# Hybrid streaming encoder step on one core: the first key and value block in another order, its weights and cached latents in smaller parts

## What is computed

```python
for l in range(DEPTH):                        # two layers; 256 prompt + 64 sample tokens
    h = rmsnorm(x, norm_mix[l]);  proj = h @ w_in[l]
    c_kv = rmsnorm(kv_lat)                    # new latents, 256 wide
    lat_all = concat([cache_latent, c_kv])    # sample stream: 512 cached rows, then 64 new
    kv = (lat_all @ w_kvup).reshape(.., 8, 64 + 64)   # per head: key part and value
    k = rmsnorm(concat([k_nope, k_rope])) * gain      # QK-norm over 96
    # attention over k and v, two other mixers, gated merge, SwiGLU
```

## Time and profile before

| What | Value |
|---|---|
| Median of 3 runs | 1054.91 us |
| Lowest and highest run | 1054.8 and 1055.82 us |
| Span of the profiled execution (the page gives no other time of it) | 1054.5 us |
| PE busy | 1046.4 us, 99% |
| DVE, ACT, POOL busy | 642.1, 503.9, 307.8 us |

### The profile page before, as it was taken

How to read it: one execution, slowest core, us unless ns; L and a number is a source line. 1 busy time by engine, 2 the same in 40 slices (tenths; PEclk the granted TensorE clock), 3 DMA queues, 4 the chain that set the end, 5 groups by cost and what they waited for, 6 DMA issues and landing times.

```text
span 1054.5 us, 20034 instructions
## 1 busy us (share of the span) xinstructions
PE 1046.4 (99%) x7594; PEld 1007.3 (96%) x7594; DVE 642.1 (61%) x1075; ACT 503.9 (48%) x915; POOL 307.8 (29%) x262
## 2 busy tenths in 40 slices
PE   8999999999999999999999999999999999999998
PEld 6899988999999999999988999989999999999998
DVE  6768764445766665643567786554457566565444
ACT  6456655444544434434354475544445444443342
POOL 2366555541121111100122755546312111111000
PEclk9999999999999999999999999999999999999999
DMA  7455433244435545454514544333355355454443
GB/s 246 117 157 147 152 96 119 94 133 148 149 113 178 159 140 153 146 181 144 177 41 137 146 146 128 99 120 104 117 160 161 120 161 158 142 156 143 156 149 122
DMA packets 49283, 147.98 MB, mean 140 GB/s; under 512 B 8865, under 2 KB 14593, under 8 KB 49217
## 3 DMA queue, kind: packets, MB, share of 16 engines
q1 hardware_dynamic: 42992, 144.76, 44.3%
q10 hardware_dynamic: 6224, 2.30, 0.9%
HBM read 143.82 MB, written 3.22 MB: 139 GB/s over the span
## 4 chain that ended last, share of the span: by engine, by line
PE 94%; DVE 3%; ACT 1%; POOL 1%; issue 1%; DMA 0%; SPq 0%; POOLq 0%; DVEq 0%; ACTq 0%
PE psum L551 28%; PE psum L553 28%; PE psum L552 28%; PE psum L703 1%; PE psum L743 1%; PE psum L726 1%; PE psum L662 1%; PE psum L734 1%; PE psum L775 1%; PE psum L663 1%; PE psum L667 1%; PE psum L950 0%; PE psum L826 0%; PE psum L641 0%; DMA raw<-w_all 0%
## 5 line engine op out<-in xcount | busy, mean ns | idle before, releaser
L551 PE MATMUL psum<-AH,WH 128*128 128x320 f32 x1328 | 415.7, 313 | 0.2
L553 PE MATMUL psum<-AH,WL 128*128 128x320 f32 x1328 | 410.3, 309 | 0.0
L552 PE MATMUL psum<-AL,WH 128*128 128x320 f32 x1328 | 410.3, 309 | 0.0
L551 PEld LDWEIGHTS psum<-AH,WH 128*128 128x128 f32 x1328 | 249.3, 188 | 7.9 <-issue 5.5
L552 PEld LDWEIGHTS psum<-AL,WH 128*128 128x128 f32 x1328 | 249.4, 188 | 0.7
L553 PEld LDWEIGHTS psum<-AH,WL 128*128 128x128 f32 x1328 | 249.3, 188 | 0.0
L1032 ACT CAST WH<-raw 128x1024 fp32r<-128x1024 f32 x167 | 174.0, 1046 | 137.2 <-PE psum L553 135.5
L1450 DVE TENSOR_TENSOR WL<-raw,WH 128x1024 fp32r<-128x1024 f32 x104 | 128.8, 1240 | 121.1 <-ACT WH L1032 120.7
L1897 POOL TENSOR_TENSOR WL<-raw,WH 128x1024 fp32r<-128x1024 f32 x61 | 149.7, 2468 | 130.1 <-ACT WH L1032 113.9
L1633 DVE TENSOR_TENSOR WL<-raw,WH 128x1024 fp32r<-128x1024 f32 x88 | 107.6, 1223 | 49.6 <-ACT WH L1195 48.2
L1902 POOL TENSOR_TENSOR fab<-fa,fb 128x320 f32<-128x320 f32 x44 | 38.7, 880 | 270.1 <-DVE fb L1638 270.1
(11 more groups left out here) (250 smaller groups left out, 1568.5 us busy)
## 6 DMA issues: line engine op xcount, KB each, us to landing
raw<-w_all SPq DMA_DIRECT2D x267, 512.0 KB, 3.5
y_out<-X SPq DMA_DIRECT2D x8, 160.0 KB, 3.0
X<-x_in SPq DMA_DIRECT2D x2, 320.0 KB, 5.5
X<-x_in SPq DMA_DIRECT2D x1, 640.0 KB, 7.2
lat_out<-ckv ACTq DMA_DIRECT2D x2, 320.0 KB, 2.9
scratch<-brel SPq DMA_DIRECT2D x8, 63.8 KB, 4.5
ckv<-lat_in SPq DMA_DIRECT2D x1, 384.0 KB, 5.5
bias<-scratch SPq DMA_DIRECT2D x8, 48.0 KB, 4.4
```

The source lines that it names most:

```text
L551: mm(out, WH[:, slot, c0:c0 + cols], high, start=first, stop=False)
L552: mm(out, WH[:, slot, c0:c0 + cols], low, start=False, stop=False)
L553: return mm(out, WL[:, slot, c0:c0 + cols], high, start=False, stop=last)
```

## The change

In block 0 of layer 0 the value rows come ahead of the key rows on PE, and their unit is loaded first, in two transfers of 512 columns. The cached rotary keys are issued ahead of the key unit, and the cached latents come in three parts (128, 128 and 256 rows) in place of two (128 and 384). ACT casts both units of `w_kvup` in halves (the key unit by its contraction halves, in strides), and PE waits for each half apart. DVE makes the value unit's low part in halves and the key unit's whole, then raises `split_ready` by two with a small memset. The third part of the latents is cast by ACT and subtracted by DVE after the keys of block 0. Unit 2 is cast by POOL (`first_cast`) in place of ACT, between the rotary parts of blocks 0 and 1. POOL's low part of unit 2 comes after block 1's rotary part, where it stood ahead of it. Layer 1 keeps its order and its two parts.

```diff
--- before.py
+++ after.py
@@ -111,6 +111,10 @@
 HALF = 64
 
 
+LATENTS = (((0, 128), (128, 256), (256, PAST)), ((0, 128), (128, PAST)))
+CKV0 = (0, 4)
+
+
 def fresh(kb):
 
     return slice(0 if kb < KB - 1 else HALF, 128)
@@ -476,11 +483,14 @@
     def _(sp):
         lat = lat_in[0:1].rearrange("a p c n -> (a p) c n")
         sp.dma_start(ckv[:, :, T:T + 128], lat[:, :, 0:128]).then_inc(s.cache_lat[0], 16)
+        sp.dma_start(raw[:, 1, 0:512], w_all[stored(1)][:, 0:512]).then_inc(s.first_raw, 16)
+        sp.dma_start(raw[:, 1, 512:1024], w_all[stored(1)][:, 512:1024]).then_inc(raw_ready[1], 16)
+        sp.dma_start(krT[64:96, T:NKEY], kr_in[0:1].rearrange("a p n -> (a p) n")).then_inc(s.cache_kr, 16)
         sp.dma_start(raw[:, 0, :], w_all[stored(0)]).then_inc(raw_ready[0], 16)
-        sp.dma_start(raw[:, 1, :], w_all[stored(1)]).then_inc(raw_ready[1], 16)
         sp.dma_start(cst[:, K_ID:K_ID + 128], cst_in[:, K_ID:K_ID + 128]).then_inc(s.id_in, 16)
-        sp.dma_start(krT[64:96, T:NKEY], kr_in[0:1].rearrange("a p n -> (a p) n")).then_inc(s.cache_kr, 16)
-        sp.dma_start(ckv[:, :, T + 128:NKEY], lat[:, :, 128:PAST]).then_inc(s.cache_lat[1], 16)
+        for n in (1, 2):
+            c0, c1 = LATENTS[0][n]
+            sp.dma_start(ckv[:, :, T + c0:T + c1], lat[:, :, c0:c1]).then_inc(s.cache_lat[n], 16)
         sp.dma_start(par[:, 0:DEPTH * NPAR], par_in).then_inc(s.par_in, 16)
         sp.dma_start(X[:, 0:2, :], x_in[:, 0:2, :]).then_inc(s.x_in[0], 16)
         sp.dma_start(raw[:, 2, :], w_all[stored(2)]).then_inc(raw_ready[2], 16)
@@ -643,25 +653,31 @@
 
         def key_rows(l, kb):
 
-            if kb == 0:
+            if kb == 0 and l > 0:
                 pe.wait_ge(s.high_ready, l * NU + U_KVK + 1)
                 pe.wait_ge(s.x_ready, 16 * l + 5)
-                pe.wait_ge(s.ckv_ready, 3 * l + 1)
+                pe.wait_ge(s.ckv_ready, CKV0[l] + 1)
             elif kb == 1:
                 pe.wait_ge(s.x_ready, 16 * l + 7)
-                pe.wait_ge(s.ckv_ready, 3 * l + 2)
+                pe.wait_ge(s.ckv_ready, CKV0[l] + 2)
             elif kb == CACHED:
                 pe.wait_ge(s.tile_free, l * NT + T_QL + 2)
-                pe.wait_ge(s.ckv_ready, 3 * l + 3)
-            elif kb != CACHED + 1:
+                pe.wait_ge(s.ckv_ready, CKV0[l] + len(LATENTS[l]) + 1)
+            elif kb > CACHED + 1 or 1 < kb < CACHED:
                 pe.wait_ge(s.kn_ready, l * KB + kb - 1)
+            if kb == 2:
+                pe.wait_ge(s.ckv_ready, CKV0[l] + len(LATENTS[l]))
             out = psum[:, kbank(kb), :]
             keys = slice(KEY0[kb], KEY0[kb] + 128)
             wh, wl = (w[:, U_KVK, :].rearrange("k (p c n) -> k c p n", p=4, c=2) for w in (WKH, WKL))
             for c in range(2):
+                if l == kb == 0:
+                    pe.wait_ge(s.first_high, 3 + c)
                 mm(out, ckvH[:, c, keys], wh[:, c], start=c == 0, stop=False)
                 mm(out, ckvL[:, c, keys], wh[:, c], start=False, stop=False)
-            if kb == 0:
+            if l == kb == 0:
+                pe.wait_ge(s.first_low, 3)
+            elif kb == 0:
                 pe.wait_ge(s.split_ready, l * NU + U_KVK + 1)
             for c in range(2):
                 last = mm(out, ckvH[:, c, keys], wl[:, c], start=False, stop=c == 1)
@@ -669,7 +685,9 @@
 
         def value_rows(l, kb):
 
-            if kb == 0:
+            if l == kb == 0:
+                pe.wait_ge(s.ckv_ready, 1)
+            elif kb == 0:
                 pe.wait_ge(s.high_ready, l * NU + U_KVV + 1)
                 pe.wait_ge(s.x_ready, 16 * l + 6)
             elif kb == 1:
@@ -681,11 +699,15 @@
             out = psum[:, kbank(kb) + 1, :]
             keys = slice(KEY0[kb], KEY0[kb] + 128)
             for c in range(2):
+                if l == kb == 0:
+                    pe.wait_ge(s.first_high, 1 + c)
                 mm(out, ckvH[:, c, keys], WKH[:, U_KVV, c * 512:c * 512 + 512], start=c == 0, stop=False)
                 mm(out, ckvL[:, c, keys], WKH[:, U_KVV, c * 512:c * 512 + 512], start=False, stop=False)
-            if kb == 0:
+            if kb == 0 and l > 0:
                 pe.wait_ge(s.split_ready, l * NU + U_KVV + 1)
             for c in range(2):
+                if l == kb == 0:
+                    pe.wait_ge(s.first_low, 1 + c)
                 last = mm(out, ckvH[:, c, keys], WKL[:, U_KVV, c * 512:c * 512 + 512], start=False, stop=c == 1)
             last.then_inc(s.v_full, 1)
 
@@ -862,8 +884,12 @@
         for l in range(DEPTH):
 
             for kb in range(CACHED):
-                key_rows(l, kb)
-                value_rows(l, kb)
+                if l == kb == 0:
+                    value_rows(l, kb)
+                    key_rows(l, kb)
+                else:
+                    key_rows(l, kb)
+                    value_rows(l, kb)
                 if kb == 0:
                     turn_rope(l, 0)
                 else:
@@ -1049,7 +1075,7 @@
 
         def cached_high(l, part):
 
-            keys = (slice(T, T + 128), slice(T + 128, NKEY))[part]
+            keys = slice(*(T + c for c in LATENTS[l][part]))
             act.wait_ge(s.cache_lat[part], 16 * l + 16)
             nc.scalar.copy(ckvH[:, :, keys], ckv[:, :, keys]).then_inc(s.ckv_cache_high, 1)
 
@@ -1205,20 +1231,30 @@
         gain_pairs = par_in.rearrange("p (l c) -> p l c", c=NPAR)[:, :, C_GQ:C_GQ + 2]
         for row, at_row in ((96, 80), (112, 64)):
             act.dma_start(gains[row:row + 16], gain_pairs[at_row:at_row + 16]).then_inc(s.gains_in, 16)
-        high(0, U_KVK)
-        high(0, U_KVV)
+        act.wait_ge(s.first_raw, 16)
+        nc.scalar.copy(WKH[:, U_KVV, 0:512], raw[:, U_KVV, 0:512]).then_inc(s.first_high, 1)
+        act.wait_ge(raw_ready[U_KVV], 16)
+        nc.scalar.copy(WKH[:, U_KVV, 512:1024], raw[:, U_KVV, 512:1024]).then_inc(s.first_high, 1)
+        act.wait_ge(raw_ready[U_KVK], 16)
+        for c in range(2):
+            h_, r_ = (w.rearrange("k (p c n) -> k c p n", p=4, c=2)[:, c] for w in (WKH[:, U_KVK, :], raw[:, U_KVK, :]))
+            nc.scalar.copy(h_, r_).then_inc(s.first_high, 1)
+        cached_high(0, 1)
 
         for l in range(DEPTH):
             if l > 0:
                 for k in range(4, KC):
                     norm_chunk(l, 0, k, square=False)
             for kb in range(CACHED):
-                key_square(l, kb)
-                if l == 0 and kb == 0:
-                    cached_high(0, 1)
-                elif l == 0 and kb < 3:
-                    high(l, U_KV + kb - 1)
-                value_copy(l, kb)
+                if l == kb == 0:
+                    value_copy(l, kb)
+                    key_square(l, kb)
+                    cached_high(0, 2)
+                else:
+                    key_square(l, kb)
+                    if l == 0 and kb == 2:
+                        high(l, U_KV + 1)
+                    value_copy(l, kb)
                 if kb == 0:
                     rope_rows(l, 0)
                     if l == 0:
@@ -1451,8 +1487,8 @@
 
         def cached_low(l, part):
 
-            keys = (slice(T, T + 128), slice(T + 128, NKEY))[part]
-            dve.wait_ge(s.ckv_cache_high, 2 * l + part + 1)
+            keys = slice(*(T + c for c in LATENTS[l][part]))
+            dve.wait_ge(s.ckv_cache_high, len(LATENTS[0]) * l + part + 1)
             TT(ckvL[:, :, keys], ckv[:, :, keys], ckvH[:, :, keys].bitcast(F32), ALU.subtract).then_inc(s.ckv_ready, 1)
 
         def full_tile(l, t):
@@ -1642,8 +1678,15 @@
         v.memset(ssum[:], 0.0).then_inc(s.warm_zero, 1)
         v.memset(par[:, DEPTH * NPAR:(DEPTH + 1) * NPAR], 0.0).then_inc(s.x_ready, KC)
         cached_low(0, 0)
-        low(0, U_KVK)
-        low(0, U_KVV)
+        for c in range(2):
+            half = slice(512 * c, 512 * c + 512)
+            dve.wait_ge(s.first_high, 1 + c)
+            TT(WKL[:, U_KVV, half], raw[:, U_KVV, half], WKH[:, U_KVV, half].bitcast(F32), ALU.subtract) \
+                .then_inc(s.first_low, 1)
+        dve.wait_ge(s.first_high, 4)
+        TT(WKL[:, U_KVK, :], raw[:, U_KVK, :], WKH[:, U_KVK, :].bitcast(F32), ALU.subtract).then_inc(s.first_low, 1)
+        dve.wait_ge(s.first_low, 3)
+        v.memset(small[:, 30:31], 0.0).then_inc(s.split_ready, 2)
         cached_low(0, 1)
 
         for l in range(DEPTH):
@@ -1652,6 +1695,8 @@
             TT(kgain[0:QK], col(C_GK, l, slice(0, QK)), col(C_GQ, l, slice(0, QK)), ALU.mult)
             for kb in range(CACHED):
                 key_scale(l, kb)
+                if l == kb == 0:
+                    cached_low(0, 2)
                 if kb == 0:
                     dve.wait_ge(s.gains_in, 32)
                     TT(kgain[QK:ROWS], gains[QK:ROWS, l, 1:2], gains[QK:ROWS, l, 0:1], ALU.mult).then_inc(s.gains, 1)
@@ -1897,6 +1942,11 @@
             g_.tensor_tensor(WL[:, u % RING, :], raw[:, u % RING, :], WH[:, u % RING, :].bitcast(F32), ALU.subtract) \
                 .then_inc(s.split_ready, 1)
```

(10 more changed lines are left out.)

5 lines of the change are left out of this document (4 added, 1 removed).

## The result

The changed kernel takes 1058.32 us in the median of 7 runs (1057.81 to 1059.8), the kernel before 1055.27 (1054.8 to 1056.65, 7 runs). The ratio is 1.003, with a 95% interval of 1.002 to 1.0039: slower by about 3 us, where I had forecast 0.5 us less and given slower 0.05. The forecast of 1054.4 and its range (to 1055.6) are both missed.

A forecast was written before the change was run, and what follows sets the result against it. PE was taken as the bound, busy 1046.4 of 1054.5 us. A lead of 1.0 at block 1's turn, cut to 0.5 by block 2's, gave 1054.0, plus 0.4: median 1054.4, range 1053.2 to 1055.6.

The forecast's parts named there:

- The opening decides, and PE's start of the dense part is the measure: Whole kernel: the change is worth what it moves PE's dense start at 24.47; some 1.8 us to be had.
- given back later: Rival, first dense part: PE waits there for ACT's squares or POOL's sums, giving 1054.9, no change; chance 0.11.
- `Kn` of block 1 comes at 16.74 - 0.4 + 0.65 = 17.0: DVE before block 1's sum: the 256-row latent part makes `Kn` 0.25 us later than before.
- it starts at 20.2: DVE's low part of unit 3 waits for POOL's low part of unit 2, starting at 20.2 instead of 19.45.
- I cost that at nothing: First dense product: low parts of `x` come up to 0.75 us later, costed at nothing, up to 0.5 without cover.
- The split costs two or three issues, but they lie 4 us ahead of the landing: Opening transfers: splitting adds no delay, and the key unit lands near 7.7.
- the key unit lands late: Rival, opening: a landing from 8.2 on makes the kernel slower, 1056.0 at half rate; chance 0.13.
- the base: Span to time: sum made against the profiled span of 1054.5, carrying 0.4 us up to the median.
- a lead of 1.3 at block 1: PE, block 1: with smaller latent parts it starts near 11.2 in place of 12.52.
- POOL's cast: Unit 2 on POOL: 1.7 us, covered by a wait; rival that it is slow gives 1057.0, chance 0.05.
- The 256-row latent part: DVE behind `Kn` of block 0: 512 elements, about 0.65 us, done by 14.9 ahead of PE's 15.35.
- The clock rises late: Rival, opening: PE's pauses keep 1.2 GHz through block 1, costing 2.8 us there, result 1055.8; chance 0.07.

The follow-up runs named there:

- run 12: Kernel before with cached latents in three parts, POOL's low part behind block 1's rotary keys, DVE's gain product and `AL` moved: 1054.74 us, ratio 0.9993.
- run 5: Changed kernel with `AL` 0 and 1 alone moved behind unit 3's low part on DVE: 1057.12 us, ratio to before 1.0013.
- run 6: Kernel before with POOL's low part of unit 2 moved behind block 1's rotary part: 1055.47 us, ratio 1.0.
- run 4: Changed kernel with DVE's second gain product moved ahead of block 0's keys and `AL` 0 and 1 behind unit 3's low part: 1055.94 us.
- run 1: Kernel before, unchanged, profiled a second time: 1055.36 us.
- run 9: Changed kernel with DVE's gain product and `AL` moved, and the key unit issued ahead of the rotary keys: 1055.79 us, ratio to before 1.0004.
- run 10: Changed kernel with DVE's gain product and `AL` moved, value unit in one transfer, key unit right behind it: 1055.14 us, ratio to before 0.9997.
- run 11: Changed kernel with only transfers altered: value unit in one transfer, key unit right behind it, rotary keys third: 1057.25 us, ratio to before 1.0017.
- run 3: Changed kernel with unit 2 cast by ACT and POOL's low part in its old place, profiled again: 1057.73 us.

## Why the prediction was wrong

**The opening decides, and PE's start of the dense part is the measure.** Right. From the first dense matmul to the end it is 1030.0 to 1030.2 us in every profile here, but for the changed kernel's 1031.5 with its 1.5 at the lower clock. Nothing was given back later: that rival falls.

**The forecast's 3.9 us of error (1058.3 for 1054.4) are 2.3 and 1.6.** The dense part was to start at 24.0 and starts at 26.28. And from span to time I carried 0.4, where every run has 2.0.

*1.5 of the 2.3: DVE's and POOL's instructions priced as if each engine were alone.* This is the step that failed: "`Kn` of block 1 comes at 16.74 - 0.4 + 0.65 = 17.0" (18.39) and, for DVE's low part of unit 3, "it starts at 20.2" (22.41). I took DVE's instructions with the durations of the old places, and weighed the low parts of `x` only as something that comes late ("I cost that at nothing"). I moved two POOL instructions without asking what DVE does beside them. The gain product went to 0.88 (0.16 in run 12, where POOL is idle): 0.7. `AL` 1 met POOL's subtraction and took 2.24, and unit 3's low part behind it started at 22.41. By run 5, where it starts 0.03 behind the end of POOL's subtraction (21.04), it could have started at 21.58: 0.8, an estimate from these rows. The second collision doesn't hang on the first, since run 6 has it alone.

Both could be read off the forecast's own times. The product follows `Kn` of block 0 by 1.5 us (15.72 - 14.24), so it would have stood near 15.1, within a cast put at 14.55 to 16.25. `AL` 1 follows `Kn` of block 1 by 1.26 (18.00 - 16.74 in the kernel before), so near 18.3, within a subtraction put at 17.75 to 20.15.

*Run 4 agrees with the forecast partly by luck.* Its `Kn` of block 1 at 16.85 and its turn of block 2 at 22.50 are the prediction's 17.0 and 22.5. But its keys were late like the changed kernel's (key cast at 8.39 for 7.7), and its edit took some 0.8 us of ordinary work (1.5 from 18.39 to 16.85, less the stall's 0.7) from ahead of block 1's sum. The two nearly cancel. Of its 2.4 us some 1.5 are the stalls; the changed kernel without these alone would be near 1056.8, by the same rows.

The rule holds in the trace of the kernel before too, where it could have been found far behind the opening. Nineteen single rows of `AL` begin there while a POOL row runs; each ends 0.34 to 0.36 behind POOL's end, and eighteen of them take 1.16 to 1.18 us. The other seven take 0.54 or 0.55, two of them with a POOL row that begins after them. Two neighbours show both cases. DVE, then POOL:

```profile
297.98 1.17 DVE L1469 SCALAR_TENSOR_TENSOR AL<-X,par,AH 128x320 fp32r<-128x320 f32 x1
...
300.34 0.55 DVE L1469 SCALAR_TENSOR_TENSOR AL<-X,par,AH 128x320 fp32r<-128x320 f32 x1 [0.70 <-ACT AH L1060]
```

```profile
297.63 1.16 POOL L1887 TENSOR_TENSOR ssum<-ssum,SQ 128x320 f32<-128x320 f32 x1 [2.36 <-ACT SQ L1064]
300.67 0.96 POOL L1887 TENSOR_TENSOR ssum<-ssum,SQ 128x320 f32<-128x320 f32 x1 [1.89 <-ACT SQ L1064]
```

Where POOL begins first, `AL` is held; where `AL` begins first, it isn't. The reverse shows as well: POOL's pair at 18.21, begun beside an `AL` that ran from 18.00 to 18.59, took 1.01 for 0.76. Not every pair fits: at 87.20 a two-input DVE subtraction (`dL`) took 0.42 within a POOL row of 86.73 to 89.23. That POOL row lasted 2.50, the same work at 81.79 took 0.28, so POOL may be the one that was held; no run settles it.

The Trainium skill states the rule ("SBUF — State Buffer", section "Who interferes with whom"): DVE and GpSimd share a pair of ports as an exclusive lock, a DVE instruction with two SBUF inputs contends with a GpSimd one that reads SBUF, a reduction never does, and issue order decides which of the two "fully blocks". The runs agree as far as they go: 2.25 for one element beside 2.42 of POOL, 1.36 for the copy, 0.49 for the sum. In its "Summary: rules for kernel authors" the same page says of such a pair to schedule "whichever is off the critical path"; `AL` and the product are off it, and run 4 takes them out of the way. It was the rule to weigh here; the prediction weighed the speed of GpSimd's cast instead.

*0.7 of the 2.3: the key unit's landing.* "The split costs two or three issues, but they lie 4 us ahead of the landing": false. The key unit was issued 0.93 later than the second unit before, and its cast came 1.05 later (8.43 for 7.38 in run 1), 0.7 later than forecast. The turn of block 0 was 0.65 late by it, and so was all behind. The mechanism was the rival "the key unit lands late", with its point of 8.2. Its cause, a halved rate, is unlikely: run 9 keeps the halves, and in its one profile the key cast starts at 7.53. Runs 10 and 11 put the worth of the other transfers at 0.8 and 1.1. How much of it is the later issue and how much the four transfers in flight together, no run separates.

*1.6: the base, the second step that failed.* I read a span of 1054.5 beside a median 0.4 above it, and carried 0.4. It is 2.0; by that, the profiled execution took some 1056.5 and was one of the longer ones. Its first block at 1.2 GHz gave me a lead of 1.3 at block 1 that most executions, by their times, don't have: in run 1 block 1 already starts at 11.43 and the dense part at 23.37. Had every other step held, the changed kernel would have taken 24.0 + 1030.0 + 2.0 = 1056.0 us, 0.7 more than the kernel before and above my range. With the collisions out, the units whole and the key unit right behind (run 10), the median is 1055.14, no gain that can be told.

**The other steps.** The values' start, near 5.9, came at 6.07, as forecast. POOL's cast took 1.50, within its bounds and near my 1.7; by itself it cost nothing, so its rival falls. The turn of block 0 waits for POOL, as I had it (0.27), but at 15.20 for 14.55. The 256-row latent part took 0.84 for my 0.65. It too has two SBUF inputs, and lies beside the end of POOL's rotary pair (15.14) and the start of its cast, so both rows may hold some waiting; no run has either alone. "The clock rises late" was right that PE's pauses matter and wrong about the place: the values ran at 2.4 GHz from 6.07 on, and the clock fell at 26.7, after a pause that DVE's stall had made. One profile shows it; a second run of the 7 has the same time and mean clock. The pause alone doesn't bring it on: in the profiles of runs 11 and 3, PE waits 1.46 us ahead of the turn of block 2 and 1.55 ahead of that of block 1, and keeps 2.4 GHz (0.15 between dense matmuls).

## What to carry to other kernels

Before moving an instruction between DVE and GpSimd, or past one on either, lay both timelines side by side and look at each pair that will overlap, in the forecast's own times. A DVE instruction with two SBUF inputs, or an fp32 copy within SBUF, that starts while a GpSimd instruction is running can last until that one ends, however small it is. A stall of DVE costs most where a chain of statistics passes through it. The cure is order, not less work: put such DVE work where GpSimd waits anyway. A trial that lands on the forecast's numbers may do so by two errors that cancel, so compare the steps ahead of them too. Profile the kernel before twice ahead of a forecast in tenths of a microsecond, and compare span and time of the same execution.
